# The last two expert pairs of a mixture-of-experts tail: the order of gate rows, down rows and scatter

## The reference, cut to what matters

```
def expert_block(args):
    xblk, e = args                        # rows of the tokens of expert e
    hid = jax.nn.silu(xblk @ w_gate[e]) * (xblk @ w_up[e])      # 1024 -> 512
    return hid @ w_down[e]                                      # 512 -> 1024
...
y = jax.ops.segment_sum(yb * row_w[:, None], row_tok, num_segments=t + 1)[:t]
...
h = h + y
return rms_norm_2(h, final_g)
```

## Time and profile before

| | |
|---|---|
| median of three runs | 1097.45 us |
| profiled execution | 1097.75 us |
| its span in the trace | 1095.8 us |
| PE busy | 1060.8 us, 97% |
| DVE, ACT busy | 617.0 us, 400.6 us |
| DMA, mean over the span | 276 GB/s |
| DMA in slices 25 to 39 of 40 (27.4 us each) | 415 to 429 GB/s |

### The profile page before, as it was taken

The page is one execution under the profiler, slowest core; times in us unless marked ns, Lnnn a source line. Parts: engine busy times, 40 slices in busy tenths (PEclk is TensorE's granted clock), DMA queues, the critical chain, the costliest instruction groups (busy, mean ns, idle before and its releaser), DMA issues.

```text
span 1095.8 us, 16973 instructions
## 1 busy us (share of the span) xinstructions
PE 1060.8 (97%) x6754; PEld 769.6 (70%) x6754; DVE 617.0 (56%) x1248; ACT 400.6 (37%) x626; POOL 6.0 (1%) x21
## 2 busy tenths in 40 slices
PE   9999999999999999999999999999999999989896
PEld 5988778998899999999889984343434344324242
DVE  4999997777568888877978763221212121112112
ACT  6512336366356555455675432010101011101012
POOL 2000000000000000000000000000000000000000
PEclk9999999999999999999999999999999999999999
DMA  8554223554244666776543789999999999999995
GB/s 303 174 164 144 99 94 106 183 167 142 77 154 158 223 241 231 251 236 207 190 152 116 269 358 420 415 426 428 428 428 427 428 428 426 427 429 428 426 423 217
DMA packets 46464, 302.58 MB, mean 276 GB/s; under 512 B 5424, under 2 KB 6576, under 8 KB 31152
## 3 DMA queue, kind: packets, MB, share of 16 engines
q1 hardware_dynamic: 42768, 286.02, 67.2%
q10 hardware_dynamic: 3616, 15.44, 4.0%
HBM read 300.39 MB, written 1.05 MB: 275 GB/s over the span
## 4 chain that ended last, share of the span: by engine, by line
PE 83%; DMA 9%; DVE 4%; ACT 2%; issue 1%; SPq 0%; DVEq 0%; ACTq 0%
PE psum L2136 82%; DMA experts_held<-in_experts 8%; DVE w_low L1242 1%; DVE arena L1242 1%; DMA x<-in_xT 1%; PE psum L2982 1%; ACT w_high L723 1%; DMA ring<-in_stream 0%; DVE x L1242 0%; DVE sq L1242 0%; DVE rt L1245 0%; ACT arena L1151 0%; PE psum L2988 0%; DVE h_low L1245 0%; SPq L533 0%
## 5 line engine op out<-in xcount | busy, mean ns | idle before, releaser
L2136 PE MATMUL psum<-experts_held,arena 128*64 128x512 f32 x992 | 220.7, 594 | 9.5 <-DMA experts_held<-in_experts 8.9
L1242 DVE TENSOR_TENSOR w_low<-ring,w_high 128x1024 fp32r<-128x1024 f32 x150 | 180.7, 1219 | 32.3 <-ACT w_high L723 31.7
L723 ACT CAST w_high<-ring 128x1024 fp32r<-128x1024 f32 x150 | 154.3, 1047 | 61.5 <-DMA ring<-in_stream 53.7
L2136 PEld LDWEIGHTS psum<-experts_held,arena 128*64 128x64 f32 x992 | 70.1, 137 | 146.7 <-issue 129.4
L2136 PE MATMUL psum<-h_high,w_high 128*128 128x256 f32 x528 | 133.0, 287 | 2.1 <-DVE h_low L1242 1.1
L2136 PE MATMUL psum<-h_low,w_high 128*128 128x256 f32 x528 | 131.1, 283 | 0.0
L1242 DVE TENSOR_TENSOR arena<-arena,psum 128x512 f32<-128x512 f32 (+1 forms) x31 | 19.3, 632 | 193.7 <-ACT arena L1151 192.9
L2136 PE MATMUL psum<-experts_held,gathered_lower 128*64 128x512 f32 x536 | 119.6, 594 | 5.4 <-DMA experts_held<-in_experts 4.4
L2136 PE MATMUL psum<-y_high,w_high 128*128 128x256 f32 x480 | 123.2, 285 | 0.5 <-DVE w_low L1242 0.4
L2136 PE MATMUL psum<-y_low,w_high 128*128 128x256 f32 x480 | 119.6, 283 | 0.0
L2136 PEld LDWEIGHTS psum<-h_high,w_high 128*128 128x128 f32 x528 | 101.2, 192 | 4.0 <-issue 1.6
(11 more groups left out here) (293 smaller groups left out, 1391.4 us busy)
## 6 DMA issues: line engine op xcount, KB each, us to landing
experts_held<-in_experts SPq DMA_DIRECT2D x73, 2048.0 KB, 33.7
ring<-in_stream SPq DMA_DIRECT2D x180, 512.0 KB, 3.4
experts_held<-in_experts SPq DMA_DIRECT2D x33, 1024.0 KB, 9.0
experts_held<-in_experts ACTq DMA_DIRECT2D x12, 1024.0 KB, 6.5
x<-in_xT SPq DMA_DIRECT2D x2, 512.0 KB, 7.5
experts_held_once<-in_experts ACTq DMA_DIRECT2D x1, 1024.0 KB, 7.3
arena<-in_memT SPq DMA_DIRECT2D x1, 512.0 KB, 8.7
bbd<-in_ssm_b SPq DMA_DIRECT2D x1, 512.0 KB, 11.7
```

What stands on the lines that cost most here:

```text
L723: act.copy(wh[:, high_slot(m)], ring[:, n_ % RING]).then_inc(hi_ready, 1)
L1242: return dve.tensor_tensor(o, a, b, op)
L2136: return pe.matmul(o, a, b, start=start, stop=stop, skip_group_check=True)
```

## The change

PE's order of the last two pairs becomes: gate rows of 14, gather of 15, `hidden_turned(14)`, scatter of 13, `scatter_turned(14)` as before; then the four **down rows of 14**; then the eight gate rows of 15, with `scatter(0)` of pair 14 behind the third and `scatter(1)` behind the fifth; then `scatter_turned(15)` and `hidden_turned(15)`; then the four down rows of 15 without a break, and the last scatter. The loads in DRAM follow that order. ACT's and DVE's programs weigh pair 14 ahead of pair 15's SiLU and product. `scatter_turned(14)` goes to `psum[5]`. The number of rows, matmuls, transposes and loads is the same. In the diff below come first the order of the loads and the bank, then ACT's, DVE's and PE's programs.

```
-GATES_AT = {p: PER_PAIR * p for p in range(PAIRS - 1)}
-GATES_AT[PAIRS - 1] = PER_PAIR * (PAIRS - 2) + 8
-DOWN_AT = {p: PER_PAIR * p + 8 for p in range(PAIRS - 2)}
-DOWN_AT.update({PAIRS - 2: LOADS - 8, PAIRS - 1: LOADS - 4})
+GATES_AT = {p: PER_PAIR * p for p in range(PAIRS)}
+DOWN_AT = {p: PER_PAIR * p + 8 for p in range(PAIRS)}
...
-            return psum[5] if p < PAIRS - 2 else dbank[0]
+            return psum[5] if p < PAIRS - 1 else dbank[0]
...
                     if p == PAIRS - 2:
                         gathered_alone(r, PAIRS - 1)
                         hidden_turned(r, p)
+                        weighed_high(r, p)
                         continue
...
                 hidden_turned(r, PAIRS - 1)
-                weighed_high(r, PAIRS - 2)
...
                         scatter_turned(r, p)
+                        weighed_low(r, p)
                         continue
...
                 hidden(r, PAIRS - 1)
-                weighed_low(r, PAIRS - 2)
                 scatter_turned(r, PAIRS - 1)
...
-                    pe.wait_ge(scwT_ready, total(r, PAIRS, p if p < PAIRS - 1 else p - 1))
+                    pe.wait_ge(scwT_ready, total(r, PAIRS, p))
...
                     ins.then_inc(expert_used, 1)
+                    if p == PAIRS - 1 and k in (2, 4):
+                        pe.wait_ge(yg_low, total(r, 2 * PAIRS, 2 * PAIRS - 3 + k // 4))
+                        scatter(k // 4)
...
                 for f in range(FE // P):
-                    if p == PAIRS - 2 and f == 2:
-                        hidden_turned(r, PAIRS - 1)
                     down_row(r, p, f, hT, dbank)
...
                         scatter_turned(r, p)
+                        downs(r, p)
                         continue
...
                 gates_and_ups(r, PAIRS - 1)
-                pe.wait_ge(scwT_ready, total(r, PAIRS, PAIRS - 1))
-                downs(r, PAIRS - 2)
+                scatter_turned(r, PAIRS - 1)
+                hidden_turned(r, PAIRS - 1)
                 pe.wait_ge(hT_ready, total(r, PAIRS, PAIRS))
-                down_row(r, PAIRS - 1, 0, last_hT, last_bank)
-                for c in range(2):
-                    pe.wait_ge(yg_low, total(r, 2 * PAIRS, 2 * PAIRS - 3 + c))
-                    scatter(c)
-                down_row(r, PAIRS - 1, 1, last_hT, last_bank)
-                scatter_turned(r, PAIRS - 1)
-                for f in range(2, FE // P):
+                for f in range(FE // P):
                     down_row(r, PAIRS - 1, f, last_hT, last_bank)
```

## The result

In 21 runs of each on the same chip the changed kernel takes 1098.0 us (median, 1097.0 to 1100.05) and the kernel before 1096.97. The ratio is 1.0014 with a 95% interval of 1.0007 to 1.002: 1.5 us slower, between 0.8 and 2.2. One execution of the kernel before was slow, at 1329.11 us, and has no part in the ratio. The two medians lie only 1.03 apart. The means of the other executions lie 1.45 apart, as the ratio has it, since a third of the changed kernel's (7 of 21) took 1099.3 to 1100.05. The forecast was +2.0, within 0.2%.

A forecast was written before the change was run, and what follows sets the result against it. PE's own sequence bounds the end, almost the landings too. 2.83 uncovered chain plus 0.20 divided scatter, less 0.58 and 0.37 transposes and 0.1 kind changes and landing wait, gives +2.0: 1099.4 us; 8-in-10 range 1096.7 to 1101.6.

The forecast's parts named there:

- (a): Pair 14's down rows moved ahead of pair 15's gate rows: no landing can become late, cost 0.
- (b): Pair 14's scatters between pair 15's gate rows: no wait for DVE; 2.24 against 2.04 us, plus 0.15 change of kind.
- (c): Pair 15's chain from gates to first down row, uncovered: 2.83 us, between 2.6 and 3.2.
- (d): Pair 15's four down rows in one piece: the third starts at 1082.2 instead of 1080.20; both orders alike from there.
- the chain costs more on an emptied PE: Between pair 15's last gate row and first down row: 3.2 not 2.83, scatters dearer; +2.5 to +2.8, 1100.1; chance 0.12.
- The clock falls: In the new gap PE's clock halves, two down rows take 3.4 us more: +5.4, 1102.9; chance 0.02.
- Landings pace both orders: Last loads 0.5 to 2 us later hold the old order, not the new: 1097.5 to 1099.0; chance 0.14.
- The chain is not uncovered: Something covers pair 15's chain between gates and down rows, so 2.83 falls out: -0.8, 1096.6; chance 0.04.

The follow-up runs named there:

- new_again: The changed kernel once more, with no edit; closing stretch (pair 14's eighth gate row to ACT's first weighing of pair 15) 40.54 us, ratio 1.0008 to the kernel before.
- new_one_piece: Changed kernel with both scatters of pair 14 in one piece behind pair 15's fifth gate row; closing stretch 40.21 us, ratio 1.0013 to the kernel before.
- old_uncovered: Kernel before with hidden_turned(15) moved straight behind pair 15's gate rows, ahead of pair 14's down rows; closing stretch 40.61 us, ratio 1.0008 to the kernel before.
- new_gap_fill: Changed kernel with pair 14's two scatters moved from between gate rows into PE's two idle times in pair 15's chain; stretch 39.83 us, ratio 0.9993 to the kernel before.
- new_late_load: Changed kernel with 1 MB (last norm's gain, written twice) put ahead of the last expert load; closing stretch 41.90 us, ratio 1.0022 to the kernel before.
- new_gap_single: new_gap_fill with three more of the stream's twos sent as single loads (LAST_SINGLE 6, not 3); closing stretch 40.01 us, ratio 1.0006 to the kernel before.

## Why the prediction was right

What was right is the mechanism and its size on PE. The sum had +2.0, the closing stretch shows +1.91 (38.68 to 40.59), and with the later traces 40.54 to 40.59 against 38.68 to 38.93, that is +1.6 to +1.9. The time as a whole rose by less: the medians by 1.03 here and by 0.89 in new_again, the ratio by 1.5. The 1098.0 us lies inside the range for 8 in 10 (1096.7 to 1101.6) but below the forecast's own range of 1098.4 to 1100.4; that the prediction holds is in part owed to how wide its range was. Step by step, the new times taken from the changed kernel's trace above:

- **(a) moved down rows.** Cost 0 was right. Four rows take 6.92 (1050.95 to 1057.87), and no row waits for a load. Its reason was not: that no landing can become late. The last one came at 38.0 rather than 36.9 after the eighth gate row; the slack took it up.
- **(b) scatters between gate rows.** Each is 1.13 (1063.12 to 1064.25, 1067.83 to 1068.96) for 1.12, and there is no wait for DVE ahead of them. From the first down row of pair 14 to the end of pair 15's gates it is 23.31, where the sum had 1075.9 - 1052.55 = 23.35. In one piece they save 0.33 to 0.38 (new_one_piece), for 0.20 and 0.15.
- **(c) the uncovered chain.** 1074.26 to 1077.08, 2.82, for 2.83. The two idle times are 1.05 and 0.68, for 1.1 and 0.8. This is the cause of the loss, shown from both sides: old_uncovered adds an idle time of 1.51 to the old order and is as much longer, less its wait for a load; new_gap_fill puts work into it and, less its waits for loads, has the old stretch of 38.6 back.
- **(d) down rows in one piece.** The third starts two rows after 1077.08, 37.7 after the eighth gate row; the sum had 1082.2 - 1044.4 = 37.8. The last row's slack is 1.4 rather than 2.6.

Of the rivals, *the chain costs more on an emptied PE* fell with 2.82. *The clock falls* did not happen in the new gap of any trace. The window of the new gap in the changed kernel, with its granted clock in the third column from the right:

```profile
1074.00:1077.00 3.00, 1.35 (x8) 0.62 (x6) 1.35 (x3) 1.16 (x2) 0.00 (x0) 1.00 0.98 407
1077.00:1080.00 3.00, 2.92 (x14) 1.06 (x16) 0.00 (x0) 0.03 (x1) 0.00 (x0) 1.00 0.59 242
```

PE is busy 1.35 of 3 us and the clock stays at 1.00, 2.4 GHz. The clock is at 1.00 there in new_again, new_one_piece and new_late_load too. The warning of the Trainium skill ("TensorE: Matmul & The Clock Gate", "HAM oscillation — how this bites in real kernels") thus didn't come true in four traces with idle times of 1.05 and 0.68 us.

But the rival is not refuted for the executions without a trace, and the prediction's argument against it was too strong. It took the clock to be at 0.50 only behind the last matmul; in the very trace that it read the clock is at 0.50 from 16 to 19 us, and the longest idle time of PE since its first matmul was 0.98. The same fall stands in new_gap_single (0.52 over 16 to 19 us), behind an idle time of 1.11; in the other twelve traces that idle time is at most 0.75 and the clock stays at 1.00. And 7 of the 21 executions of the changed kernel and 2 of the 11 of new_again have a mean granted clock of 0.995 or 0.996. These nine took 1099.31 to 1100.05; the other 23, at 0.997 or 0.998, 1097.0 to 1098.61. Of the kernel before, 6 of the 102 executions whose clock is on record in the later runs are at 0.996 or below. None of the 22 executions of the order with both gaps filled is, but 4 of the 11 of new_gap_single are. Where in the execution the clock fell isn't recorded without a trace. It may be in the new gap, or early, as in the two traces that show it.

*Landings pace both orders* forecast 1097.5 to 1099.0, and 1098.0 is in that range too. Its condition isn't met in the three traces of the old order, which waits at most 0.2 us there; but it is a true mechanism: with the last load 2 to 3 us later the two kernels tie. *The chain is not uncovered* is refuted by the brackets at 1075.74 and 1077.08.

What stays open is the way from the stretch to the whole time. Executions at a mean clock of 0.997 or 0.998 have medians of 1097.76 (changed) and 1097.67 (new_again), and 1096.83 for the kernel before in the series of new_again: 0.8 to 0.9 apart, where the stretch says 1.6 to 1.9. The same gap shows in new_gap_fill, whose stretch is 0.9 to 1.2 longer than the old one and whose median is 0.4 lower. The start of the eighth gate row could hold a part of it. Without the two traces whose clock fell early it lies between 1042.4 and 1043.2 in the seven traces of the new orders and between 1042.7 and 1043.7 in the five of the old ones, which is too few to tell. So of the +2.0 that was forecast, some 0.8 to 1.5 us are shown in the whole time, and about 1 us of what the stretch shows is not found again there.

## What to carry to other kernels

Before taking work out from between a producer chain and its consumer, list what then stands on the bounding engine between the two: here the down rows that were moved were the cover of a chain of 2.8 us, and of all steps of a large edit that was the one that counted. A gap that such a chain leaves can be filled with small independent pieces, here 2.3 us of work for 0.2, but look first at how much later the bounding engine may finish before the data stream becomes the limit. To see an effect of 0.2% compare from a common event in both traces, not the spans: it repeated to 0.05 us in the changed kernel, where the times scattered by 3. But hold it against the medians as well, and against which executions the traces are of: here half of the loss seen in the stretch didn't come through to the median.

## What the runs showed of the hardware that I had not expected

TensorE's clock can fall without a long pause. In two of the fourteen traces, the kernel before and new_gap_single, it is 0.50 and 0.52 over 16 to 19 us, and PE's longest idle time since its first matmul was 0.98 and 1.11; those two executions have a mean clock of 0.996 and reach the eighth gate row at 1044.43 and 1043.93, later than all twelve others (1042.4 to 1043.7). In four traces two pauses of 1.05 and 0.68 near the end left it at 1.00.

The last loads, issued at the same place in all (3.6 to 3.7 us after the start of the eighth gate row), took 33.2 to 33.5 us to land in three traces of the old order and 33.7 to 34.9 in six of new ones and in old_uncovered. SP's next issue, of the last norm's gain, lasts 4.24 us in those three and 4.7 to 5.5 in the seven. All of the lateness comes in at one load of 2 MB, which lands 14.6 to 14.9 us after the eighth gate row in the three traces and 15.1 to 16.2 in the seven, and why is not known.
